# Moving the gate weights of a two-slot expert group from ScalarE to VectorE, with new group positions

## The reference, cut to what matters

```python
q = (xb @ w_q).reshape(128, 8, 2, 128)
s = einsum('tphd,phnd->tphn', q, subkeys)          # scores against 128 + 128 subkeys
s1, i1 = top_k(s[:, :, 0], 16); s2, i2 = top_k(s[:, :, 1], 16)
cand = s1[..., :, None] + s2[..., None, :]         # 256 candidates, top 16 of them
g = softmax(top)
act = gelu(einsum('tped,td->tpe', u[eidx], xb), approximate=False)
out = einsum('tpe,tped->td', g * act, v[eidx])
```

## Time and profile before

| what | us |
|---|---|
| median of 3 runs | 2443.47 |
| lowest, highest | 2439.6, 2455.03 |
| profiled execution (the highest of the three) | 2455.03 |
| its span from first to last instruction | 2453.2 |

### The profile page before, as it was taken

One profiled execution on the slowest core, in us unless ns is written; L12 is line 12 of the kernel. 1 busy time (PEld: TensorE's weight loads), 2 busy tenths in 40 slices (PEclk: granted clock), 3 DMA queues, 4 the chain that ended last, 5 costly groups with the idle time before them and its releaser, 6 DMA issues. The chain is left out here.

```text
span 2453.2 us, 24295 instructions
## 1 busy us (share of the span) xinstructions
PE 1888.2 (77%) x6858; PEld 1105.0 (45%) x6858; DVE 1754.5 (72%) x4165; ACT 831.0 (34%) x2507; POOL 907.7 (37%) x772
## 2 busy tenths in 40 slices
PE   7986886887987766586987677889798667766675
PEld 6774563665643333253643254546464223322232
DVE  2346887676758777656678768987776898776765
ACT  2313343433322322344323234443323234222232
POOL 0012432333533333332444414544344444444441
PEclk9997897988998888798998888899899888888888
DMA  9958988899999999999999989999999999999996
GB/s 388 408 137 354 378 337 327 346 367 413 402 417 419 418 418 418 420 389 422 391 418 420 421 310 421 420 407 402 384 412 420 415 421 421 422 421 421 421 422 255
DMA packets 159145, 958.25 MB, mean 391 GB/s; under 512 B 20260, under 2 KB 22948, under 8 KB 60708
## 3 DMA queue, kind: packets, MB, share of 16 engines
q0 software_dynamic: 110592, 805.36, 79.7%
q1 hardware_dynamic: 42032, 147.02, 15.5%
q10 hardware_dynamic: 6388, 4.33, 0.9%
HBM read 953.75 MB, written 2.89 MB: 390 GB/s over the span
## 5 line engine op out<-in xcount | busy, mean ns | idle before, releaser
L749 POOL DMA_INDIRECT rows<-in_uv,eidx x768 | 907.5, 1182 | 1503.8 <-PE acc L829 979.3
L829 PE MATMUL acc<-rows,diag 128*128 128x512 f32 x2268 | 1154.8, 662 | 317.3 <-ACT diag L1026 312.4
L1338 DVE CUSTOM_DVE_ANT_0 rows<-rows,xb 128x1024 f32<-128x1024 f32 x768 | 911.7, 1221 | 259.9 <-DMA rows<-in_uv,eidx 250.5
L829 PEld LDWEIGHTS acc<-rows,diag 128*128 128x128 f32 x2268 | 466.6, 213 | 923.4 <-issue 527.1
L1026 ACT ACTIVATE act_out<-act_in 128x2 f32<-128x2 f32 x384 | 77.5, 202 | 959.7 <-DVE act_in L1338 915.9
L1314 DVE SCALAR_TENSOR_TENSOR side<-rows,wv,side 128x1024 f32<-128x1024 f32 x201 | 258.1, 1284 | 54.6 <-ACT wv L1026 48.7
L1026 ACT ACT_TABLE_LOAD x127 | 162.9, 1283 | 301.4 <-DVE act_in L1338 222.4
L767 PE MATMUL bank<-wt,hT 128*128 128x256 f32 x928 | 211.9, 389 | 11.3 <-ACT hT L1026 8.2
L1026 ACT ACTIVATE diag<-small,wv 128x128 f32<-128x128 f32 x567 | 207.8, 397 | 12.5
L767 PEld LDWEIGHTS bank<-wt,hT 128*128 128x128 f32 x928 | 181.6, 196 | 45.5 <-ACT hT L1026 9.0
L1026 ACT ACTIVATE wv<-act_out,gate 128x1 f32<-128x1 f32 x768 | 184.3, 287 | 12.6
(11 more groups left out here) (178 smaller groups left out, 1284.5 us busy)
## 6 DMA issues: line engine op xcount, KB each, us to landing
wt<-in_ada_w SPq DMA_DIRECT2D x63, 512.0 KB
wt<-in_peer_w_q SPq DMA_DIRECT2D x48, 512.0 KB
rows<-in_ada_w SPq DMA_DIRECT2D x33, 512.0 KB, 15.4
wt<-in_mlstm_w_in SPq DMA_DIRECT2D x27, 512.0 KB
rows<-in_uv,eidx POOLq DMA_INDIRECT x768
wt<-in_attn_w_qkv SPq DMA_DIRECT2D x24, 512.0 KB
rows<-in_mlstm_w_in SPq DMA_DIRECT2D x21, 512.0 KB, 16.1
rows<-in_peer_w_q SPq DMA_DIRECT2D x16, 512.0 KB, 13.3
```

The costliest lines, as they stand in the source:

```text
L749: nc.gpsimd.indirect_dma_start(out=rows[:, r, :], out_offset=None, in_=A["uv"], in_offset=bass.IndirectOffsetOnAxis(ap=eidx[:, b, slot:slo ...
L829: last = nc.tensor.matmul(acc[:, h * 512:(h + 1) * 512], diag[:, DIAGS.index((ring, j)), :], rows[:, r, D + h * 512:D + (h + 1) * 512], st ...
L1338: last = V.tensor_tensor_reduce(out=rows[:, r, 0:D], in0=rows[:, r, 0:D], in1=xb[:, place, :], scale=1.0, scalar=0.0, op0=ALU.mult, op1=AL ...
```

## The change

- ACT no longer multiplies with the gates. DVE has a new function `weigh`: it waits for the Gelu of a group and multiplies both values with both gates in one instruction (128x2), `wv` with semaphore `weighted` as before. In a stretch DVE weighs group n-1 after the dots of group n, ahead of the side add of n-1. The last group of a stretch is weighed when the next stretch opens, or at once at the end of an order (`finish`).
- ACT does the Gelu of group n, and makes the diagonals of group n-1 behind it; where a stretch opens, it makes those of n-1 ahead of the Gelu. The last group of an order gets its diagonals at the end of its stretch (`last_groups`). ACT's waits for its own Gelu and for the gates (`gated`) go, and DVE's wait for its own dots ahead of a side add.
- `DEALS` of the orders (0,0) and (1,0) is written anew. In (0,0) the stretches go from 35 to 38 and those of a single group from 14 to 19, in (1,0) from 35 to 37 and from 18 to 20. The running total of groups at a step moves by -4 to +2 in (0,0) and -3 to +2 in (1,0). At MLQK of the sample it goes from 5 to 3, at the step behind it (MLG) it stays 7.

PE, POOL and SP keep their instructions; only the places of the groups move. The hunks that merely drop `gated` from the lists of names are left out.

```diff
--- before.py
+++ after.py
@@ -70,8 +70,8 @@
 
 
 DEALS = {
-    (0, 0): [1, 0, 0, 0, 2, 0, 0, 2, 2, 1, 3, 2, 0, 0, 0, 3, 0, 1, 0, 1, 0, 2, 1, 2, 0, 3, 0, 0, 0, 0, 1, 1, 3, 0, 0, 1, 1, 0, 2, 0, 0, 0, 2, 0, 0, 3, 0, 0, 0, 1, 2, 1, 1, 2, 0, 0, 2, 3, 3, 2, 0, 0, 0, 0, 1, 1, 0, 2, 0, 0, 0, 0, 0, 0, 0, 0, 3],
-    (1, 0): [0, 0, 1, 0, 0, 3, 4, 0, 3, 3, 0, 2, 0, 1, 1, 2, 1, 1, 4, 0, 1, 1, 1, 1, 2, 0, 2, 1, 1, 1, 2, 0, 1, 1, 3, 1, 1, 2, 2, 4, 0, 1, 0, 0, 2, 2, 0, 0, 1, 4],
+    (0, 0): [1, 0, 0, 0, 1, 0, 0, 1, 4, 0, 1, 3, 2, 0, 0, 2, 1, 0, 0, 1, 0, 2, 1, 1, 0, 3, 0, 1, 1, 0, 1, 2, 2, 0, 0, 1, 1, 0, 2, 0, 0, 0, 2, 0, 0, 1, 0, 2, 0, 0, 3, 0, 0, 4, 0, 0, 2, 2, 1, 1, 0, 0, 2, 0, 2, 0, 0, 2, 0, 0, 0, 0, 0, 2, 1, 1, 1],
+    (1, 0): [0, 0, 1, 0, 1, 2, 3, 2, 2, 2, 0, 2, 1, 0, 1, 2, 3, 1, 3, 1, 1, 1, 2, 1, 1, 0, 1, 1, 0, 2, 1, 1, 2, 1, 1, 1, 2, 1, 4, 1, 0, 0, 2, 0, 4, 1, 0, 0, 0, 5],
 }
 
 
...
@@ -662,13 +662,7 @@
 
                 return place["chain"]
 
-            def gated(order, quarter):
-
-                l, b = GORDER[order]
-                g = "S" if b else "P"
-                return before[PLAN.index(("PG", l, g, BLOCKS[g].index(b), quarter)) + 1][4]
-
-            return begin, of, tile, full, by, emptied, next_of, one, noted, gated
+            return begin, of, tile, full, by, emptied, next_of, one, noted
 
         def weight_place(i):
 
...
@@ -1044,22 +1038,23 @@
                 act.wait_ge(mean_sq, next_of(mean_sq))
                 f(sd[:, 0:n], ms[:, 0:n], ACT.Sqrt).then_inc(root, 1)
 
-            def group(order, n, slot, ring, turn, g, opens):
-
-                b = GORDER[order][1]
-                if g is not None and (opens or g % (GROUPS // QUARTERS) == 0):
-                    act.wait_ge(dve_step, gated(order, g // (GROUPS // QUARTERS)))
-                act.wait_ge(dots, n + 1)
-                f(act_out[:, ring, :], act_in[:, ring, :], ACT.Gelu).then_inc(gelus, 1)
-                act.wait_ge(gelus, n + 1)
-                for j in range(GS):
-                    share = gate[:, b, slot + j:slot + j + 1] if isinstance(slot, int) else gate[:, b, bass.ds(slot + j, 1)]
-                    last = f(wv[:, ring, j:j + 1], act_out[:, ring, j:j + 1], ACT.Copy, scale=share)
-                last.then_inc(weighted, 1)
+            def diagonals(order, n, ring, g):
+
                 act.wait_ge(weighted, n + 1)
                 for j in range(GS - has_side(order, ring, g)):
                     last = f(diag[:, DIAGS.index((ring, j)), :], ident, ACT.Copy, scale=wv[:, ring, j:j + 1])
                 last.then_inc(diags, 1)
+
+            def group(order, n, slot, ring, turn, g, opens):
+                if opens and g != 0:
+                    diagonals(order, n - 1, (ring - 1) % RING, None if g is None else g - 1)
+                act.wait_ge(dots, n + 1)
+                f(act_out[:, ring, :], act_in[:, ring, :], ACT.Gelu).then_inc(gelus, 1)
+                if not opens:
+                    diagonals(order, n - 1, (ring - 1) % RING, None if g is None else g - 1)
+
+            def last_groups(order, n):
+                diagonals(order, n - 1, (n - 1) % RING, GROUPS - 1)
 
             def store(out, in_):
                 act.dma_start(out, in_).then_inc(stored, 16)
...
@@ -1082,7 +1077,7 @@
                 if dves:
                     act.wait_ge(dve_step, dves)
                 if k == "GROUPS":
-                    run_groups(act, s, group, lambda order, n: None)
+                    run_groups(act, s, group, last_groups)
                     continue
                 if noted():
                     act.wait_ge(act_chain, noted())
...
@@ -1308,6 +1303,12 @@
                         last.then_inc(dve_chain, one())
                 last.then_inc(dve_step, 1)
 
+            def weigh(b, n, slot, ring):
+
+                dve.wait_ge(gelus, n + 1)
+                g = gate[:, b, slot:slot + GS] if isinstance(slot, int) else gate[:, b, bass.ds(slot, GS)]
+                V.tensor_tensor(wv[:, ring, :], act_out[:, ring, :], g, ALU.mult).then_inc(weighted, 1)
+
             def add_up(n, ring):
 
                 dve.wait_ge(weighted, n + 1)
...
@@ -1318,14 +1319,13 @@
 
             def finish():
 
-                for order, n, ring in left:
+                for b, order, n, slot, ring in left:
+                    weigh(b, n, slot, ring)
                     if has_side(order, ring, n % GROUPS):
-                        if side_sums(n):
-                            dve.wait_ge(side_summed, side_sums(n))
                         add_up(n, ring)
                 left.clear()
 
-            def group(place):
+            def group(b, place):
                 def body(order, n, slot, ring, turn, g, opens):
                     if opens:
                         finish()
...
@@ -1340,8 +1340,8 @@
                                                       accum_out=act_in[:, ring, j:j + 1])
                     last.then_inc(dots, 1)
                     if not opens:
+                        weigh(b, n - 1, slot - GS, (ring - 1) % RING)
                         if has_side(order, (ring - 1) % RING, None if g is None else g - 1):
-                            dve.wait_ge(dots, n + 1)
                             add_up(n - 1, (ring - 1) % RING)
                 return body
 
...
@@ -1366,11 +1366,11 @@
                     if s[3] == 0:
 
                         dve.wait_ge(experts_chosen, QUARTERS * GORDER.index((s[1], s[2])) + 1)
-                    run_groups(dve, s, group(GORDER.index((s[1], s[2])) % 2), lambda order, n: None)
+                    run_groups(dve, s, group(s[2], GORDER.index((s[1], s[2])) % 2), lambda order, n: None)
                     _, l, b, lo, hi = s
                     order = GORDER.index((l, b))
                     n = order * GROUPS + hi - 1
-                    left.append((order, n, n % RING))
+                    left.append((b, order, n, (hi - 1) * GS, n % RING))
                     if hi == GROUPS:
                         finish()
                     continue
```

More of the change, by code:

```diff
@@ L756, in _ @@
         def _(pe):
-            begin, of, tile, full, by, emptied, next_of, one, noted, gated = places("P")
+            begin, of, tile, full, by, emptied, next_of, one, noted = places("P")
             used = [0]
@@ L1021, in _ @@
         def _(act):
-            begin, of, tile, full, by, emptied, next_of, one, noted, gated = places("A")
+            begin, of, tile, full, by, emptied, next_of, one, noted = places("A")
             sent = {"stored": 0, "state_out": 0}
@@ L1273, in _ @@
         def _(dve):
-            begin, of, tile, full, by, emptied, next_of, one, noted, gated = places("D")
+            begin, of, tile, full, by, emptied, next_of, one, noted = places("D")
             V = nc.vector
```

## The result

The changed kernel is slower: 2485.53 us, median of 4 runs (2484.05 to 2486.57), against 2445.93 for the kernel before, beside it (4 runs, 2439.6 to 2455.03). The ratio is 1.0163, 95% interval 1.013 to 1.0196: about 40 us. In all 17 executions of the changed kernel on record the times run from 2475.9 to 2497.46, with a median of 2486.06, so a difference of a few us between two medians of four says little. The predicted time was 2442, the range 2410 to 2464.

The account below looks back on a forecast made before the run. No engine was full; gathers set the pace over most of the second half, the PE, DVE and ACT chain in stages 1 and 4. Terms: -10, +2.4, +3, +3, in all -1.6; from the median 2443.47 to 2442 us, range 2410 to 2464.

Parts of the forecast that it names:

- Groups dealt anew: New group positions in stages 1 and 4: -4 us at the sample's second NT and MLQK, 0 for other shifts.
- one place: Stage 1, sample's second NT to MLQK: one group ahead instead of two, MLG reached with the same 7; -4 us.
- the other places: Remaining shifts of one or two groups both ways, taken as 0 us; they could be -20 or +8.
- bounds of -20 and +8: What shifts of one or two groups, aside from the place worked out, could bring, in us; 0 was taken.
- Stage 1 at 431, stage 4 at 392: Stage lengths in us expected in the new profile, stage 1 give or take 8.
- The weights, weighing and new waits: Stages 1 and 4: ACT's weights go (-8.2, -2, -2.8), DVE's weighing comes (+3.2, +3.0), DVE waits for Gelu (+1, +1).
- Later diagonals: Diagonals made one group later: ring places come free 4.4 us later where PE is level with DVE; +3 us taken.
- +3 at the ring: Ring places freed later in about five dips of the gathers: between 0 and 22 us, 3 taken.
- +3 and +1.2 at ends: PE adds two groups after the last dots: kernel's end +1.5 to +7, +3 taken; end of order (0,2) +1.2.
- B: DVE becomes the pace in stages 1 and 4, every weighing on the path: 2468 us; chance 0.1.
- C: The ring starves: all five dips get 4.4 us deeper and cost it in full, 2461 us; chance 0.1.
- A: Hand-dealt stages 1 and 4 win back 40% of 80 us as positions fit the quicker ACT: 2411 us; chance 0.2.

Follow-up runs that it names:

- e1: The changed code with the group positions of the kernel before in both hand-dealt orders: 2438.73 us against 2447.72, ratio 0.9961.
- e15: The changed kernel with two groups of stage 4 moved from behind the step PQ to ahead of it: 2486.83 us, ratio 1.0162.
- e18: The changed kernel with the old list of stage 4 up to the first 46 of its 64 groups: 2474.41 us, ratio 1.012.

## Why the prediction was wrong

**The step that failed is "Groups dealt anew".** It was priced at -4 us from one place and 0 "at the other places". Measured, the two lists cost +32 us in the old code and, from 0.9961 to 1.0163, about +49 in the new one. The one place was right as far as it went: MLQK comes 4.5 us earlier. But PE doesn't reach MLG "with the same 7 groups" for nothing: it makes 24 records (10.46 us) there instead of 12 (5.31 us), and MLG is 0.6 us late. The gain was moved, not made. The "0 elsewhere" took displacements of one or two groups both ways to cancel. They don't: in stages 3 and 4 a list that is nowhere later than the old one loses 19 us (775 against 756), and a tail that is later at most steps loses 15. What each step's delay does to the gathers was never worked out from the lists. The warning at the prediction's end, that places other than the one worked out could do much more, was the right one; its bounds of -20 and +8 were not drawn from any row.

**Stage 1 at 431, stage 4 at 392.** They are 442 and 407. With the new code and old lists they are 427 and 377; of the 377, some 10 us are the moved boundary of stage 3, and the sum of the two is 756 against 757 before. The 441 us taken as the base of stage 1 held 11.26 us of waiting for the state's load that most executions probably lack.

**The weights, weighing and new waits** (-8.2, -2, -2.8, +3.2, +3.0, +1, +1: together -5 us) are worth -15 by difference of the two runs with the old lists, or about -8 if the kernel with ratio 0.999, which differs from e1 only in PE's order at PS, is taken. By the stage lengths without the wait for the load (433 to 427, and 757 to 756 for stages 3 and 4) it is -6 in stage 1, where these terms add up to -6, and -1 in stages 3 and 4, where they add up to +1.2. So the sign was right; whether the size was too small isn't shown. The weighing itself came out as sized: 155 ns where 158 was taken. Side adds no longer wait (7.1 us against 54.6).

By the table of the Trainium skill (VectorE: DVE Perf Modes, The TRN2 errata) such a product would take 63 ns; the trace has more than twice that. The same section of the Trainium skill also gives (N + 151) / 0.96 ns for an fp32 tensor_tensor add. Taken for this product with N = 2 that is 159 ns, an estimate from that figure; the trace agrees with it, at 155. The prediction had passed over that figure.

**Later diagonals** (+3 at the ring, +3 and +1.2 at ends: 7.2) measured +6 us alone. POOL's waits don't show the term at the ring. In the changed kernel it waits 1076.6 us for PE where it waited 979.3, but that has the new lists in it. With old lists and the diagonals later alone it waits 1059.1 us for PE and 13.6 for DVE's side adds, together 1072.7, and before 979.3 and 101.8, together 1081.1. By stages, with the diagonals later alone, stage 1 takes 433 us and stage 6 363, against 429 and 359 in the kernel before without the load and its wait; the others agree within 1 us. At the end of the kernel the last Gelu starts at 2466.20 and the sum is read at 2475.47, 9.27 us later, where it was 5.12: +4.1, within the 1.5 to 7 given. The twelve products ran as one piece (changed kernel, last sums of PE and the read by DVE):

```profile
2467.04 8.19 PE L823 MATMUL acc<-rows,diag 128*128 128x512 f32 x12 [3.23 <-ACT diag L1020]
...
2475.47 1.22 DVE L1750 TENSOR_TENSOR arena<-acc,side 128x1024 f32<-128x1024 f32 x1 [7.55 <-PE acc L823]
```

**The rivals.** B (DVE becomes the pace) isn't it: DVE is busy 323 of 442 and 304 of 407 us. The prediction took the Trainium skill's advice to work on the engine with the highest occupancy (Perfetto Trace Analysis, Identifying the Most-Contended Engine) as speaking for B. The run of the code alone gives that reading no support: loading DVE, busy 72%, to relieve ACT didn't make the kernel slower (0.9961). C (the ring starves) came nearest, but with the wrong cause and place: it asked for stages 2, 3 or 5 below 405 GB/s by the later diagonals, and these stand at 411 to 417. The gathers did stop, in stages 1 and 4, by the positions. A took the new lists to fit the quicker ACT; they cost time with the old code and with the new.

## What to carry to other kernels

A hand-made order of work is a change of its own: price it apart from the code that comes with it, and test it apart, because here it turned a small gain (0.1 to 0.4%) into a 1.6% loss. When positions move, count for every step what was freed before it, not only what the step no longer waits for, and follow the chain past the step that gains: here the next one paid. Before a wait in one profiled execution enters the base of a sum, ask whether every execution has it.

## What the hardware did that I had not expected

The 512 KB load of the state, queued beside the gathers, has two durations. From its first packet to its last it took 6.7 to 8.6 us in nine of the profiled kernels and 18.1 to 20 us in nine others (before and after among the latter), with little between, and a kernel isn't tied to one of them: the changed kernel took 19.6 us, and e15 and e18, which have the same list and code up to there, 8.5 and 8.4 us. In the long case PE waits 9.3 to 11.3 us, and the gathers stop behind it, since nothing frees the ring. What decides between the two wasn't tested; with the new code the long case came only with the new positions of stage 1 (8 profiles of 10, against none of 5).
